# Combining the experts' rows: two blocks by one-hot products, gathers and weighting begun in the last block, one root for both norms, a branch that falls through

## What is computed

```python
out = jnp.zeros((T + 1, D), yb.dtype).at[buf_tok].add(yb * buf_w[:, None])[:T]   # two expert rows a token
x = x + gt2 * out
x = rms_norm(x, g_final)                     # end of the first block
h = jnp.concatenate([meta, x], axis=1)       # 16 learned rows ahead of the tokens
hn = _rmsnorm(h, norm_mix_pre)
proj = hn_p @ w_in                           # start of the second block
```

## Time and profile before

| | us |
|---|---|
| median of 3 runs | 1842.43 |
| the three runs | 1841.90, 1842.43, 1845.53 |
| span of the profiled execution | 1839.2 |
| the profiled execution's own time | its span and what lies around it, not recorded apart; the median is 3.23 above the span |
| PE busy in the span | 1735.8 (94%) |
| DVE busy | 813.6 (44%) |
| ACT busy | 592.7 (32%) |
| granted TensorE clock, mean | 0.988 |

### The profile page before, as it was taken

How to read it: one execution, slowest core, us unless ns; L and a number is a source line. 1 busy time by engine, 2 the same in 40 slices (tenths; PEclk the granted TensorE clock), 3 DMA queues, 4 the chain that set the end, 5 groups by cost and what they waited for, 6 DMA issues and landing times. The chain is left out here.

```text
span 1839.2 us, 27607 instructions
## 1 busy us (share of the span) xinstructions
PE 1735.8 (94%) x11694; PEld 1325.7 (72%) x11694; DVE 813.6 (44%) x1409; ACT 592.7 (32%) x1007; POOL 59.8 (3%) x86
## 2 busy tenths in 40 slices
PE   6999999999999999879998999999999999999997
PEld 2884445666656555539765888899998899999886
DVE  3874656411111111244386577352246554444333
ACT  4433432100000000037687434552323333222322
POOL 1001000000000000010000000000000000000000
PEclk9999999999999999989999999999999999999999
DMA  9765733899999999962110011132232033322321
GB/s 371 273 207 157 282 107 128 358 427 427 427 427 427 427 426 426 427 247 92 58 47 24 24 47 47 47 115 92 92 115 69 17 119 100 98 92 92 115 69 46
DMA packets 110629, 348.85 MB, mean 190 GB/s; under 512 B 8587, under 2 KB 71329, under 8 KB 97191
## 3 DMA queue, kind: packets, MB, share of 16 engines
q1 hardware_dynamic: 105910, 337.59, 48.1%
q0 software_dynamic: 4224, 9.31, 1.4%
q10 hardware_dynamic: 370, 0.14, 0.0%
HBM read 323.92 MB, written 23.07 MB: 189 GB/s over the span
## 5 line engine op out<-in xcount | busy, mean ns | idle before, releaser
L1837 PE MATMUL psum<-parts_memory 128*128 128x256 f32 (+3 forms) x1088 | 330.8, 304 | 13.5 <-issue 4.7
L1838 PE MATMUL psum<-parts_memory 128*128 128x256 f32 (+3 forms) x1088 | 327.7, 301 | 0.0
L1839 PE MATMUL psum<-parts_memory 128*128 128x256 f32 (+3 forms) x1088 | 327.2, 301 | 0.0
L1736 DVE TENSOR_TENSOR parts_memory<-fixed,parts_memory 128x1024 fp32r<-128x1024 f32 x139 | 167.2, 1222 | 194.1 <-ACT parts_memory L1728 192.0
L1837 PEld LDWEIGHTS psum<-parts_memory 128*128 128x128 f32 x1088 | 206.5, 190 | 25.6 <-issue 12.5
L1839 PEld LDWEIGHTS psum<-parts_memory 128*128 128x128 f32 x1088 | 206.7, 190 | 6.9
L1838 PEld LDWEIGHTS psum<-parts_memory 128*128 128x128 f32 x1088 | 206.3, 190 | 6.9
L1837 PE MATMUL psum<-mix_parts,parts_memory 128*128 128x256 f32 (+2 forms) x664 | 205.2, 309 | 1.1 <-DVE mix_parts L3197 0.7
L1838 PE MATMUL psum<-mix_parts,parts_memory 128*128 128x256 f32 (+2 forms) x664 | 206.2, 311 | 0.0
L1839 PE MATMUL psum<-mix_parts,parts_memory 128*128 128x256 f32 (+2 forms) x664 | 205.3, 309 | 0.0
L1728 ACT ACTIVATE parts_memory<-fixed 128x1024 fp32r<-128x1024 f32 x139 | 143.4, 1056 | 109.9 <-PE psum L1839 109.7
(11 more groups left out here) (473 smaller groups left out, 2530.8 us busy)
## 6 DMA issues: line engine op xcount, KB each, us to landing
fixed<-in_w_exp_gate_dram SPq DMA_DIRECT2D x19, 2048.0 KB, 24.8
fixed<-in_w_exp_up_dram SPq DMA_DIRECT2D x19, 2048.0 KB, 22.7
fixed<-in_w_in_dram SPq DMA_DIRECT2D x36, 1024.0 KB, 8.5
fixed<-in_w_exp_down_dram SPq DMA_DIRECT2D x18, 2048.0 KB, 26.7
attention_memory<-in_w_exp_down_dram SPq DMA_DIRECT2D x14, 2048.0 KB, 27.3
attention_memory<-in_w_exp_up_dram SPq DMA_DIRECT2D x13, 2048.0 KB, 25.0
attention_memory<-in_w_exp_gate_dram SPq DMA_DIRECT2D x13, 2048.0 KB, 23.5
fixed<-in_w_mod_dram SPq DMA_DIRECT2D x8, 2048.0 KB, 9.1
```

The source lines that it names most:

```text
L1736: dve.tensor_tensor(out, raw, high.bitcast(F32), ALU.subtract).then_inc(self.low_ok, 1)
L1837: pe.matmul(out, x(0), w(0), start=start, stop=False)
L1838: pe.matmul(out, x(0), w(1), start=False, stop=False)
L1839: return pe.matmul(out, x(1), w(0), start=False, stop=stop)
```

## The change

Six edits, all at this seam:

1. The last **two** blocks' rows (31 and 32, `OWN` = 2) go by one-hot products; DVE builds two matrices in block 29, PE turns eight tiles after block 30 and has four products per t instead of two. Block 31 is no longer stored.
2. The gathers wait for the store of block 30, for the gate product of block 31 and for the arrival of the last up weights, and no more for block 31's store.
3. ACT's `prepare_act` runs ahead of the last block's Silu, and a new `prepare_dve` ahead of its `hidden`; both wait for the three loads. DVE weights the rows of t = 0 (`weight_rows`) between `take_h` and `take_y` of the last block.
4. The residual is multiplied by the final gain alone (`scaled`), both sums of squares are taken, and one root serves the second norm: with least = EPS * (mean of squares + EPS) as its bias it gives the root for the scaled rows. The first norm's own factor is applied to the residual at the end, by four ACT copies.
5. PE and DVE have an If whose first body is the combine, so that no branch is taken into it; the further blocks and a copy of the combine stand in the Else.
6. SP's first loads of the second block's weights also wait for the last down weights.

```diff
@@ Routing: places in the last two blocks
-        step(dve.tensor_scalar(own, dest_at, -float(LAST * BR), None, ALU.add))
-        step(dve.tensor_scalar(dest_early, dest_at, float(LAST * BR), None, ALU.min))
+        for j in range(OWN):
+            step(dve.tensor_scalar(own[:, j, :], dest_at, -float((LAST - j) * BR), None, ALU.add))
+        step(dve.tensor_scalar(dest_early, dest_at, float(FIRST_OWN * BR), None, ALU.min))
@@ POOL
-            for b in range(LAST):
+            for b in range(FIRST_OWN):
                 store(b, b % Y_SLOTS)
...
+            pool.wait_ge(w_read, reads_of(LOADS - 6))
+            pool.wait_ge(w_in[(LOADS - 2) % EXPERT_SLOTS], 16 * ((LOADS - 2) // EXPERT_SLOTS + 1))
             gather(pool)
@@ PE
-            n = blocks_more(pe)
-            loop(pe, n, more_rows)
-            combine_pe(pe, n)
+                    further = blocks_more(pe)
+            with pe.If(further < 1):
+                combine_pe(pe)
+                pe.nop()
+            with pe.Else():
+                further_turns(pe, further, more_rows)
+                pe.wait_ge(g["added_more"], 2 * TT)
+                combine_pe(pe)
+                pe.nop()
@@ ACT
             for b in range(FIRST_MORE):
+                if b == LAST:
+                    prepare_act(act)
                 gate(b)
...
-            prepare_act(act)
@@ DVE
                 if b == EXPERTS - BATCH + 1:
                     choose_own()
+                    n = blocks_more(dve)
+                if b == LAST:
+                    prepare_dve(dve)
                 hidden(b)
                 take_h(b)
+                if b == LAST:
+                    weight_rows(dve, 0)
                 take_y(b)
@@ combine: SP
+        sp.wait_ge(g["expert_arrived"][(LOADS - 1) % EXPERT_SLOTS], 16 * ((LOADS - 1) // EXPERT_SLOTS + 1))
@@ combine: DVE, in finish_dve
         def add(t):
...
-        def last_norm(t):
-            dve.wait_ge(root, t + 1)
-            step(dve.reciprocal(rstd[:, t:t + 1], rstd[:, t:t + 1]))
-            dve.scalar_tensor_tensor(out=res[:, t, :], in0=res[:, t, :], scalar=rstd[:, t:t + 1], in1=gfin,
-                                     op0=ALU.mult, op1=ALU.mult).then_inc(x3, 1)
+            dve.wait_ge(mixed, 2 * t + 1)
+            dve.tensor_tensor(scaled[t], res[:, t, :], gfin, ALU.mult).then_inc(mixed, 1)
+        def least_variance(t):
+            dve.wait_ge(ssq, t + 1)
+            dve.tensor_scalar(least[:, t:t + 1], ss[:, t:t + 1], EPS, EPS, ALU.add, ALU.mult).then_inc(least_ok, 1)
@@ combine: ACT
     def prepare_act(act):
         act.wait_ge(loads, 48)
-        act.wait_ge(g["w_read"], 3 * FIRST_MORE - 1)
-        second_half(act, -1)
+        act.wait_ge(g["w_read"], reads_of(LOADS - 5))
+        pre_root(act, -1)
...
         take(4)
+        act.wait_ge(least_ok, TT + 1)
+        for t in range(TT):
+            act.activation(res[:, t, :], scaled[t], ACT.Copy, scale=rstd[:, t:t + 1])
@@ combine: PE, in mix(t)
-            for half in range(2):
-                rows = slice(BR * half, BR * half + BR)
-                last = pe.matmul(psum[:, bank + half, :], g["own_rows"][rows, t * P:(t + 1) * P], g["own_y"][rows, :],
-                                 start=(t < BY_VECTOR), stop=True)
+            for j in range(OWN):
+                for half in range(2):
+                    rows = slice(BR * half, BR * half + BR)
+                    last = pe.matmul(psum[:, bank + half, :], g["own_rows"][j][rows, t * P:(t + 1) * P], g["own_y"][j][rows, :],
+                                     start=(t < BY_VECTOR and j == 0), stop=(j == OWN - 1))
...
+        turn(0)
         mix(0)
         mix(1)
-        turn(0)
         pe.wait_ge(hn_low, 2)
```

More of the change, by code:

```diff
@@ L1287, in experts @@
     Y_STORE = 16
-    yb = [late[:, o:o + 512] for o in (7184, 15888)]
-    Y_SLOTS = len(yb)
+    yb = [late[:, o:o + 512] for o in (7184, 15888)] + [arena[:, 3072:3584]]
+    Y_SLOTS, Y_MORE = 2, 2
     BX, BG, BU, BH, BY = 0, 2, 3, 4, 5
@@ L1296, in wait, with loop @@
             eng.wait_ge(sem, value)
-    def loop(eng, n, body, tail=None):
+    def loop(eng, n, body):
         with eng.If(0 < n):
@@ L1306, in loop, with further_turns @@
                     eng.nop()
-            if tail:
-                tail()
+            eng.nop()
+        eng.nop()
+    def further_turns(eng, n, body):
+        body(1)
+        with eng.If(1 < n):
+            with eng.Fori(1, MORE - 1) as i:
+                with eng.If(i < n):
+                    body(i + 1)
+                eng.nop()
             eng.nop()
@@ L1591, in take_y @@
                 dve.wait_ge(w_read, b * 3 + 3)
-                j, stored = stored_before(b)
-                wait(dve, y_st[j], stored)
-                if not isinstance(b, int):
+                j = Y_MORE
+                if isinstance(b, int) and b < FIRST_MORE:
+                    j, stored = stored_before(b)
+                    wait(dve, y_st[j], stored)
+                elif not isinstance(b, int):
                     dve.wait_ge(y_more, b * 32 - 32 * FIRST_MORE)
@@ L1652, in _ @@
                     last_route_dve(dve)
-            n = blocks_more(dve)
-            loop(dve, n, more_rows, lambda: mix_more(dve))
-            combine_dve(dve)
+            with dve.If(n < 1):
+                combine_dve(dve)
+                dve.nop()
+            with dve.Else():
+                further_turns(dve, n, more_rows)
+                mix_more(dve)
+                combine_dve(dve)
+                dve.nop()
+            dve.nop()
 RAW_SLOTS, RAW = 3, 2048
@@ L1943, in mix_more, with prepare_dve, weight_rows @@
             dve.wait_ge(added_more, i + 1)
-    added_more = sem("further_rows_added")
+    added_more = g["added_more"] = sem("further_rows_added")
+    def prepare_dve(dve):
+        dve.wait_ge(loads, 48)
+        dve.wait_ge(root2, 1)
+        dve.reciprocal(rstd2[0:META, 0:1], rstd2[0:META, 0:1]).then_inc(dstep, 1)
+        dve.wait_ge(dstep, 1)
+        dve.scalar_tensor_tensor(out=meta[0:META, :], in0=meta[0:META, :], scalar=rstd2[0:META, 0:1], in1=gpre[0:META, :],
+                                 op0=ALU.mult, op1=ALU.mult).then_inc(hn_ok, 1)
+    def weight_rows(dve, t):
+        dve.wait_ge(y_in[t], 32)
+        for k in range(2):
+            i = 2 * t + k
+            dve.scalar_tensor_tensor(out=res[:, t, :], in0=y[:, i, :], scalar=weight[:, i:i + 1], in1=res[:, t, :],
+                                     op0=ALU.mult, op1=ALU.add).then_inc(dstep, 1)
+            dve.wait_ge(dstep, i + 2)
     def finish_dve(dve):
-        step = Steps(dve, dstep)
+        step = Steps(dve, dstep, 1 + 2 * BY_VECTOR)
         def add(t):
@@ L1979, in low_rows @@
                 dve.tensor_tensor(out, src, high.bitcast(F32), ALU.subtract).then_inc(hn_low, 1)
-        dve.wait_ge(loads, 48)
-        pre_norm(-1)
-        for t in range(BY_VECTOR):
-            dve.wait_ge(y_in[t], 32)
-            for i in (2 * t, 2 * t + 1):
-                step(dve.scalar_tensor_tensor(out=res[:, t, :], in0=y[:, i, :], scalar=weight[:, i:i + 1], in1=res[:, t, :],
-                                              op0=ALU.mult, op1=ALU.add))
+        weight_rows(dve, 1)
         add(0)
         low_rows(0)
+        least_variance(0)
+        add(1)
         parts.low(dve, Q_AT)
-        add(1)
-        last_norm(0)
-        last_norm(1)
+        least_variance(1)
         pre_norm(0)
@@ L2008, in finish_dve @@
         low_rows(4)
+        dve.wait_ge(root, 1)
+        dve.reciprocal(rstd, rstd).then_inc(least_ok, 1)
     def squares_of(act, src, out, n, done, count):
```

133 lines of the change are left out of this document (74 added, 59 removed).

## The result

The changed kernel takes **1852.22 us** (median of 4 runs, 1850.26 to 1853.5) against 1842.16 (4 runs beside it): ratio 1.0056, 95% interval 1.0032 to 1.008. The profiled span went from 1839.2 to 1850.5 us.

A forecast was written before the change was run, and what follows sets the result against it. Bound by weight loads until about 795, then by a combine chain over all engines up to the barrier. Terms + 15.1 - 8.6 + 1.15 + 0.3 + 2.9 = + 10.8 on 1842.4 give 1853.2 us; range 1847.0 to 1861.0.

The forecast's parts named there:

- G: Time the last of the three small loads lands: about 800.5 predicted, between 797.95 (as before) and 804.3.
- (a): Last block: the last Silu, now behind squares, root and table loads, ends at G + 4.45; before, it ran at 788.84.
- (b): Last block: PE idles some 11 us, resumes at half clock; last down product ends at G + 13.75, + 15.1 us.
- the prediction's last paragraph: Signs to look for in the changed profile, among them PE's clock at half for some 10 us from about 798.
- (c): Last down product's end to the products of t = 2: 6.3 us instead of 14.90, a gain of 8.6.
- (d): Products of t = 2 to the projection: 11.92 against 10.77 us to the turns, + 1.15; shorter norm chain gains nothing.
- (e): Projection to its last product: VectorE's norm of t = 2 takes 7.9 against 7.7 us; + 0.3 with t = 3.
- (f): Barrier: four ACT copies behind VectorE's last split and a reciprocal make ACT end at 847.2, + 2.9 us.
- (g): Block 29: second matrix overruns VectorE's slack by up to 2.2 us, covered by PE's DMA waits; uncovered, 2 to 3.
- 1 (not slower): Last block: G at 789.3 or earlier, before the Silu needs it; 1841.4 or, tail hidden, 1838.5 us; chances 0.09, 0.06.
- Rival 3: Combine: the untaken branch doesn't help, PE's stalls of 3.90 and 4.34 us stay; 1860.4 us, chance 0.07.
- Rival 2: Behind the last product: PE's jump over the Else stalls once more, 4.34 us; up to 1857.5 us, chance 0.15.

The follow-up runs named there:

- prepare_late: Changed kernel with ScalarE's learned-row preparation put back behind the last Silu and VectorE's behind the last take_y: 1845.61 us, ratio 1.0022 to the kernel before.
- no_tail: Changed kernel without the four ACT copies that apply the first norm's factor to the residual: 1850.17 us, ratio 1.0045 to the kernel before.
- loads_early: Changed kernel with the loads of the learned rows and the first norm's gains issued ahead of expert 24's weights: 1843.9 us, ratio 1.0019 to the kernel before.
- before_branch_only: Kernel before with only the If and Else on PE and VectorE, and an If around ScalarE's further blocks: 1841.06 us, ratio 0.9996.
- loads_early_copies_spread: As loads_early, with the four residual copies spread: one ahead of the last evictions, two behind, one on VectorE: 1841.2 us, ratio 1.0009 to the kernel before.
- jump_inside: As loads_early_copies_spread, with the no-further-blocks branch ending earlier, where PE and VectorE wait anyway: 1838.44 us, ratio 0.9987 to the kernel before.
- gathers_held: As loads_early_copies_spread, with the gathers and the next stage's first weight loads held until the last down product is done: 1850.77 us, one run.

## Why the prediction was right

The time (1853.2 predicted, 1852.22 measured) and the mechanism hold: the move of the preparation costs 7.3 us by itself, and undoing it gives back 6.6. That the sum came so close is luck in part; by the distances from the last up product:

- **G.** Predicted 800.5, measured 801.63, or 799.8 without the 1.87. From the start of the up product it is 7.85 to 7.89 us in the three kernels that gather late and 9.62 to 9.78 in the three that gather early with the loads unmoved (changed, prepare_late, no_tail): the early gathers cost the load some 1.8 us, where I had 2.5. The share of two thirds for the older queue was thus about right.
- **(a)** G + 4.45 predicted, 806.08, that is G + 4.45, measured.
- **(b)** G + 13.75 predicted, G + 12.03 measured: the mis-sized term. I had the clock come back 8.4 us after the PE resumed, as at 808.50 before; it came 5.2 after (806.59 to 811.8). The low stretch as a whole is 13.7 us long in both (803.2 to 816.9 and 798.2 to 811.8), where the prediction's last paragraph has some 10. One case of the clock's return is no figure for the next. With G this makes + 12.6 in place of + 15.1.
- **(c)** - 8.6 predicted, 6.2 in place of 14.90, so - 8.7, measured.
- **(d)** + 1.15 predicted, + 0.3 measured (834.83 - 819.87 against 828.70 - 814.07). I added two rows of 1.13 for each tile; but the records of neighbours overlap, and from the first of such a pair to the row behind both it is 1.92 (823.50 to 825.42). From the products of t = 2 to the turns it is 11.10, not 11.92. That the shorter norm chain gains nothing is borne out: turn to projection is 3.86 in both.
- **(e)** + 0.3 predicted; projection to the end of its last product is 15.23 against 15.46: - 0.2.
- **(f)** + 2.9 predicted, + 3.0 measured (3.93 against 0.92), though not for the whole reason: of it 1.96 are the copies' own and 1.05 would stay without them (no_tail).
- **(g)** The second matrix overran VectorE's slack in block 29 by some 1.3 (the hidden product at 750.30 against 747.25, less the run's shift), and the next block's wait for weights absorbed it, as predicted.
- **Missing:** 2.2 us of half clock behind the barrier. The PE idles 4.40 there, and the sum ends at the barrier as if the idle time had no effect behind it.

So 12.6 - 8.7 + 0.3 - 0.2 + 3.0 = 7.0 at the barrier, where I had 10.8, and + 2.2 behind it, 9.2; the error of 3.8 in the terms and the missing 2.2 partly cancel. The medians differ by 10.1 (1852.22 against 1842.16).

Of the rivals, 1 (not slower) failed as the argument against it said: G was 10 to 12 us too late for it. Its condition was met once the loads were issued ahead of expert 24's weights (loads_early: the Silu at 792.20 waits for the PE), but that kernel was still slower (1.0019); its time of 1838.5 was reached only with the copies spread and the jump moved (1838.44). Rival 3 (the stalls stay) failed: no such idle time is left in the changed kernel, and 0.89 with the branches alone. Rival 2 (the branch is paid at the end) was right in kind and small in size: 1.27 us at the barrier in before_branch_only, 1.05 in no_tail, 1.07 between loads_early_copies_spread and jump_inside, all hidden under ScalarE's copies in the changed kernel. The profile's DMA queues show that code was fetched. Over 848 to 856, in the changed kernel:

```profile
q8 instruction: 3, 0.05, 2.7%
```

while the kernel before has no packet of that queue over 840 to 848. In jump_inside, one packet of it falls in 823 to 826.3, where the PE waits anyway, and none in 841 to 843. The Trainium skill ("Runtime: NRT & Kernel Launch", instruction fetch mechanics) has a taken branch stall where its target is outside the pages already fetched; the trace agrees for the jump over the Else, and adds the size: 1.05 to 1.3 us with the DMA engines quiet, against 3.90 and 4.34 with gathers under way.

## What to carry to other kernels

Before an early step is moved ahead of a step on the path, read when its *inputs* land, and move their loads first: here the same reordering cost about 7 us with the loads late, and with them moved the kernel was no slower than with the preparation put back (ratios 1.0019 and 1.0022). A jump is best placed where its engine waits anyway; here that and the clock behind it were worth 1.2 + 1.7 us in the profiled executions. A barrier is to be priced by the idle time of the PE in it, with what the clock takes behind it.

## What the runs showed of the hardware

- **The clock behind a barrier.** With 1.40 to 1.42 us of idle time there (three kernels) the clock stayed whole and the stretch to the pair of copies took 18.34 to 18.39; with 2.44 to 4.40 (seven kernels) it fell to 0.50 (1.2 GHz), in some before and in some after the PE had resumed, and the stretch took 19.77 to 21.81. One microsecond more of idle time cost up to 3.4 (no_tail). Its length does not follow the idle time: the low clock lasted 6.8 us behind 4.40, 4.38 and 2.44, and 3.4 behind 4.38, 2.67, 2.54 and 2.47; why stays open.
- **The clock inside the stage.** Behind the same idle time of 1.90 us ahead of the projection it fell to 0.50 for 3.4 us in five kernels (changed, no_tail, loads_early_copies_spread, jump_inside, gathers_held) and stayed whole in the other five. So the length of an idle time alone does not decide, and what does stays open.
- **VectorE can stand still** where no row names a wait while transfers are under way: 3.75 to 3.77 us ahead of its copy in the last block in four kernels with gathers and loads under way, 0.78 with them held (one run); what it waits for stays open.
